# Latent products in another order, and finer waits in front of two output products, in a two-block transformer kernel

## What is computed

```python
proj = x @ w_in[l]        # na_q, na_k, na_v, df_q, df_k, df_v, m_cq (384), m_ckv (256), m_kr (32), gates
na_out  = neighbourhood_attention(...)              # 8 heads
df_out  = diff_attention(...)                       # 4 heads, two softmaxes each
q  = rms_norm(m_cq,  q_norm_g)  @ w_mla_qb          # latent attention, 8 heads
kv = rms_norm(m_ckv, kv_norm_g) @ w_mla_kvb         # gives k_nope and v
k  = concat(k_nope, rope(m_kr))
mla_out = softmax(rope(q) @ k.T * scale) @ v
merged = sum(sigmoid(gate_b) * (out_b @ w_branch[b]) for b in 0..2)
x = layer_norm(ALPHA * x + merged @ w_out)
hidden = silu(x @ w_gate) * (x @ w_up)              # 2816 wide
x = layer_norm(ALPHA * x + hidden @ w_ffn_out)
```

## Time and profile before

| | |
|---|---|
| median of 3 runs | 3397.44 us (3393.65 to 3398.08) |
| the profiled execution's own time | 3403.85 us |
| its span | 3402.0 us |
| mean granted TensorE clock | 0.966 of full |
| TensorE busy | 3179.8 us, 93% |
| VectorE, ScalarE, GpSimd busy | 41%, 31%, 10% |
| TensorE waiting for VectorE line 2703 / 2722 / 2579 (hidden) | 15.6 / 9.2 / 4.6 us, twice each |

### The profile page before, as it was taken

How to read it: one execution, slowest core, us unless ns; L and a number is a source line. 1 busy time by engine, 2 the same in 40 slices (tenths; PEclk the granted TensorE clock), 3 DMA queues, 4 the chain that set the end, 5 groups by cost and what they waited for, 6 DMA issues and landing times.

```text
span 3402.0 us, 38118 instructions
## 1 busy us (share of the span) xinstructions
PE 3179.8 (93%) x15140; PEld 2264.7 (67%) x15140; DVE 1388.2 (41%) x1857; ACT 1071.4 (31%) x1787; POOL 339.3 (10%) x269
## 2 busy tenths in 40 slices
PE   6989999979999979989999899998998999899996
PEld 3867777844444438765777688786775678678874
DVE  5676443341111054644334533334554433543334
ACT  3245332221001024445333322213444433232212
POOL 2455020000000011102100000000211110000000
PEclk9988999979999999999999999998999999999998
DMA  6012443459999942110212223233120122222221
GB/s 218 25 50 73 158 142 106 154 203 409 409 409 409 409 161 75 59 55 26 69 63 93 72 90 99 77 98 78 60 64 25 56 62 87 81 81 92 92 85 59
DMA packets 266257, 436.76 MB, mean 128 GB/s; under 512 B 9696, under 2 KB 180192, under 8 KB 265312
## 3 DMA queue, kind: packets, MB, share of 16 engines
q1 hardware_dynamic: 266080, 434.32, 36.2%
HBM read 432.19 MB, written 2.10 MB: 128 GB/s over the span
## 4 chain that ended last, share of the span: by engine, by line
PE 55%; DVE 5%; ACT 2%; DVEq 1%; issue 1%; ACTq 0%; POOLq 0%; DMA 0%; SPq 0%
PE bank L2247 46%; PE bank L2308 2%; PE bank L2325 2%; PE bank L2344 1%; PE bank L2284 1%; PE bank L1895 1%; DVE ring_r L2579 1%; PE bank L2339 1%; ACT ring_r L2448 1%; PE bank L2314 1%; DVE x L1926 1%; DVE layers_norm_rstd L1923 0%; DVE layers_work L2698 0%; DVE x_r L1937 0%; POOLq L2760 0%
## 5 line engine op out<-in xcount | busy, mean ns | idle before, releaser
L2247 PE MATMUL bank<-experts_x_hi_r,ring_r 128*128 128x512 f32 x1720 | 576.7, 400 | 7.0 <-DVE ring_r L2579 7.0
L2247 PE MATMUL bank<-x_r,ring_r 128*128 128x512 f32 x1376 | 546.2, 397 | 0.0
L2579 DVE TENSOR_TENSOR ring_r<-ring,ring_r 128x2048 fp32r<-128x2048 f32 (+2 forms) x162 | 324.9, 2006 | 421.0 <-ACT ring_r L2448 420.1
L2448 ACT ACTIVATE ring_r<-ring 128x2048 fp32r<-128x2048 f32 (+2 forms) x162 | 272.7, 1683 | 494.0 <-PE bank L2247 475.7
L2247 PE MATMUL bank<-layers_work_r,ring_r 128*128 128x512 f32 x1312 | 392.3, 401 | 9.2 <-DVE layers_work_r L2722 9.2
L2247 PEld LDWEIGHTS bank<-experts_x_hi_r,ring_r 128*128 128x128 f32 x1720 | 324.2, 188 | 109.5 <-issue 25.2
L2247 PE MATMUL bank<-ring_r 128*128 128x512 f32 (+1 forms) x1224 | 387.1, 377 | 0.0
L2247 PEld LDWEIGHTS bank<-layers_work_r,ring_r 128*128 128x128 f32 x1312 | 249.4, 190 | 78.6 <-DVE layers_work_r L2722 10.1
L2247 PEld LDWEIGHTS bank<-x_r,ring_r 128*128 128x128 f32 x1376 | 259.1, 188 | 62.9 <-issue 1.0
L2770 POOL TENSOR_TENSOR layers_p<-layers_p,layers_recip 128x512 f32<-128x512 f32 (+2 forms) x160 | 145.3, 925 | 1445.8 <-DVEq L2625 1445.8
L2247 PEld LDWEIGHTS bank<-ring_r 128*128 128x128 f32 x1224 | 223.5, 188 | 46.8
(11 more groups left out here) (399 smaller groups left out, 4827.1 us busy)
## 6 DMA issues: line engine op xcount, KB each, us to landing
ring<-in_w_in SPq DMA_DIRECT2D x74, 1024.0 KB, 5.3
ring<-in_w_ffn_in SPq DMA_DIRECT2D x44, 1024.0 KB, 5.1
mixer_kept<-in_w_up SPq DMA_DIRECT2D x33, 1024.0 KB, 18.3
mixer_kept<-in_w_down SPq DMA_DIRECT2D x28, 1024.0 KB, 18.5
mixer_kept<-in_w_gate SPq DMA_DIRECT2D x27, 1024.0 KB, 18.5
ring<-in_w_gate SPq DMA_DIRECT2D x24, 1024.0 KB, 18.4
ring<-in_w_down SPq DMA_DIRECT2D x23, 1024.0 KB, 18.4
ring<-in_w_ffn_out SPq DMA_DIRECT2D x32, 704.0 KB, 4.5
```

The lines of the kernel that those rows point to most:

```text
L2247: last = pe.matmul(out, lhs, rhs, start=start and k == 0, stop=stop and k == len(pairs) - 1)
L2448: act.activation(r32(whole(key, hi_at(i, key))), whole(key, raw_at(i, key)), ACT.Identity).then_inc(slab_round, 1)
L2579: dve.tensor_tensor(r32(tile), tile, r32(hi), ALU.subtract).then_inc(done, 1)
```

## The change

Three edits, in both layers.

1. The latent fills come in another order: features 4, 5, 3, 2, then msq kv, then features 0 and 1, the swap of the rotary key, msq q, then mv 0 and on as before. The slabs of these features are loaded in the order 2, 1, 0. msq kv waits for two squares instead of five, msq q for five. mv 0 waits for two of latent_done, and a new wait for all five stands before qn 0. The q root moves from tile 6 to tile 10 (mv 0 writes tile 6), and VectorE counts the roots in the new order. The events around a unit keep their places: a fill of the same number stands in the same slot. msq kv and feature 0 now follow the scores of unit (df, 2, 1), feature 1 and the swap those of (df, 2, 2), msq q and mv 0 those of (df, 2, 3).
2. wo 0 waits for six merged blocks, does their 18 passes, waits for all eight and does the last six passes.
3. fo 0 waits for 11 hidden blocks, and for all 22 in front of its second half.

```diff
--- before.py
+++ after.py
@@ -1970,7 +1970,8 @@
         v = toks("dfv", hh)
         return [a[0], a[1], q[0], b[0], q[1], b[1], k[0], v[0], k[1], v[1], v[2], v[3]]
 
-    latent = [("feat", "lat", m) for m in range(6)] + [("msq", "q"), ("msq", "kv"), ("swap", "kr", 0)]
+    lat = lambda *which: [("feat", "lat", m) for m in which]
+    latent = lat(4, 5, 3, 2) + [("msq", "kv")] + lat(0, 1) + [("swap", "kr", 0), ("msq", "q")]
     latent += [("mv", t) for t in range(TT)] + [("flip",), ("qn", 0), ("kn", 0), ("qr", 0), ("kn", 1), ("swap", "qr", 0)]
     queries = [("qn", 1), ("qr", 1), ("qn", 2), ("qn", 3), ("swap", "qr", 1), ("kn", 2), ("kn", 3)]
 
@@ -2019,7 +2020,7 @@
          "qn": (12, 14, 15, 18), "qr": (13, 10), "kn": (16, 17, 19, 21),
          "merged": (0, 1, 2, 3, 4, 20, 22, 23), "heads_hi": (24, 25, 26, 27), "merged_hi": (6, 7, 8, 9, 12, 13, 14, 15)}
 LAMBDA_AT = ("tok", "nav", 0, 0)
-LATENT_ROOT = {"q": 6, "kv": 9}
+LATENT_ROOT = {"q": 10, "kv": 9}
 WORK = 28
 
 
@@ -2103,7 +2104,7 @@
     source = {}
     for g, names in enumerate((("naq", "nak", "nav"), ("dfq", "dfk", "dfv"))):
         source |= {(n, hh): (W, 0, D, 512 * (3 * g + k) + 256 * hh, 256) for hh in (0, 1) for k, n in enumerate(names)}
-    source |= {("lat", c): (W, 0, D, L0 + 256 * c, 256) for c in range(3)}
+    source |= {("lat", c): (W, 0, D, L0 + 256 * c, 256) for c in (2, 1, 0)}
     source |= {("mla", 0): ("w_mla_2", 0, 3 * 768), ("mla", 1): ("w_mla_2", 3 * 768, 2 * D)}
     for b in range(3):
         for c in range(4):
@@ -2259,15 +2260,19 @@
                     return [(r32(a), r32(b)) for k in range(len(lhs))
                             for a, b in ((lhs[k], rhs[k]), (lhs[k], rhs_lo[k]), (lhs_lo[k], rhs[k]))]
 
-                def by_feature(key, c0, rhs, rhs_lo):
+                def by_feature(key, c0, rhs, rhs_lo, late=None):
 
                     slab = slabs_of(key)[0] if key[0] != "fu" else ("ffn", key[1])
                     need(slab)
                     hi, lo = parts(i, slab)
                     n = hi.shape[1]
                     banks.vacant(pe, key, i)
-                    chain(core.ps(key)[:, :], three([hi[:, k, c0:c0 + P] for k in range(n)], [lo[:, k, c0:c0 + P] for k in range(n)],
-                                                    rhs, rhs_lo)).then_inc(banks.put(key), 1)
+                    pairs, at = three([hi[:, k, c0:c0 + P] for k in range(n)], [lo[:, k, c0:c0 + P] for k in range(n)], rhs, rhs_lo), 0
+                    if late is not None:
+                        at = 3 * (n - 2)
+                        chain(core.ps(key)[:, :], pairs[:at], stop=False)
+                        pe.wait_ge(*late)
+                    chain(core.ps(key)[:, :], pairs[at:], start=at == 0).then_inc(banks.put(key), 1)
 
                 def couple(keys, fresh):
 
@@ -2387,11 +2392,13 @@
                         last.then_inc(banks.put(e), 1)
                     elif kind == "msq":
                         first, n, mat = (0, 3, "mean_q") if e[1] == "q" else (3, 2, "mean_kv")
-                        pe.wait_ge(latent_squared, i * LATENT + first + n)
+                        pe.wait_ge(latent_squared, i * LATENT + (2 if e[1] == "kv" else LATENT))
                         emit(e, [c2(mat)] * n, [tile("latent_sq", first + j) for j in range(n)])
                     elif kind in ("mv", "qn", "qr", "kn"):
                         need(("mla", 0), ("mla", 1))
                         if e == ("mv", 0):
+                            pe.wait_ge(latent_done, i * LATENT + 2)
+                        if e == ("qn", 0):
                             pe.wait_ge(latent_done, i * LATENT + LATENT)
                         wq, wkv = (flat[:, raw_at(i, ("mla", j)):raw_at(i, ("mla", j)) + n].rearrange("p (k n) -> p k n", k=k)
                                    for j, n, k in ((0, 3 * 768, 3), (1, 2 * D, 2)))
@@ -2410,9 +2417,9 @@
                                    [heads_out[:, e[1], k, :] for k in range(4)])
                     elif kind == "wo":
                         if e[1] == 0:
-                            pe.wait_ge(merged_split, i * KD + KD)
+                            pe.wait_ge(merged_split, i * KD + KD - 2)
                         by_feature(e, (e[1] % 2) * P, [tile("merged_hi", m) for m in range(KD)],
-                                   [tile("merged", m) for m in range(KD)])
+                                   [tile("merged", m) for m in range(KD)], (merged_split, i * KD + KD) if e[1] == 0 else None)
                     elif kind == "norm":
                         if e[1] == 1:
                             need()
@@ -2421,12 +2428,14 @@
                         by_feature(e, P * (kind == "fu"), x_hi, xs)
                     elif kind == "fo":
                         if e[1] == 0:
-                            pe.wait_ge(hidden_split, i * KF + KF)
+                            pe.wait_ge(hidden_split, i * KF + KF // 2)
                         banks.vacant(pe, e, i)
                         for hh in (0, 1):
                             need(("fo", e[1], hh))
                             hi, lo = parts(i, ("fo", e[1], hh))
                             n = KF // 2
+                            if e[1] == 0 and hh == 1:
+                                pe.wait_ge(hidden_split, i * KF + KF)
                             last = chain(core.ps(e)[:, :], three([hi[:, k, :] for k in range(n)], [lo[:, k, :] for k in range(n)],
                                                                  [hidden_hi(hh * n + k) for k in range(n)],
                                                                  [hidden(hh * n + k) for k in range(n)]),
@@ -2693,7 +2702,7 @@
                             dve.tensor_tensor(dst, dst, ssq[:, n, :].unsqueeze(2).broadcast_to([P, DF_HEADS, P]), ALU.mult)\
                                .then_inc(levelled, 1)
                     elif kind == "msq":
-                        dve.wait_ge(latent_root_done, i * 2 + (e[1] == "kv") + 1)
+                        dve.wait_ge(latent_root_done, i * 2 + (e[1] == "q") + 1)
                         root = work_tile(LATENT_ROOT[e[1]])
                         dve.reciprocal(root, root)
                         dve.drain()
```

## The result

The changed kernel takes 3368.62 us (median of four runs, 3366.52 to 3372.88) against 3397.4 for the one before (four runs): a ratio of 0.9919, 95% interval 0.9906 to 0.9931, or 27.5 us less with the interval 23 to 32; the two medians lie 28.8 us apart. The forecast was 3364.9, in a range of 3354 to 3381. The profiled execution of the changed kernel is the longest of its four, 3372.88 with a span of 3371.1 and a mean granted clock of 0.969 (before: 3403.85, span 3402.0, clock 0.966).

What follows compares the result with a forecast made beforehand. TensorE, busy 93% of the span, was taken as the bound, so only its gaps and half-clock stretches count. 18.7 + 8.9 + 4.9 = 32.5 us off the 3397.44 median gave 3364.9, range 3354 to 3381.

Steps and rivals of the forecast that it cites:

- The latent stage: Wait before the first latent product (mv) goes; 21.9 us available less two new waits of 1.6: gain 18.7, bounds 15.3 and 21.9.
- The combine at s + 11.9: VectorE ends unit (df, 2, 2)'s combine 11.9 us after s, the end of unit (df, 2, 3)'s scores on TensorE.
- I take nothing for the shorter gap: Latent stage: no clock loss counted behind the new 1.5 us gap at the transposes; 1.7 us each kept as other end.
- s + 5.30: Old trace's latent stage: VectorE's reciprocal starts 5.30 us after a unit's scores end, table load ahead of q root already counted.
- The first output product: Starts 2.81 us earlier, leaving a 1.8 us gap and a free second wait; 4.5 per layer, 8.9 us, bounds 5.6 and 10.6.
- I take half, 0.85: First output product: the remaining 1.8 us gap loses 1.7 us of clock or nothing, so 0.85 is counted per layer.
- The first down product: Its 2.28 us wait goes altogether, 2.4 with pipeline fill, with no clock lost: 4.9 us in both layers.
- A: Latent stage's q root binds harder and clocks drop, also at the output products: gain 24.6, 3372.8 us; chance 0.24.
- B: Latent wait only moved: transposes wait 5.5 us for the q part plus clock 2.7; gain 19.3, 3378 us; chance 0.08.
- C: Slower: granted clock falls because TensorE rests less; a fall of 0.03 gives 3421 us; chance 0.03.
- D: Edits don't act: another semaphore or bank releases TensorE at the same time; within 0.2%, 3397 us; chance 0.05.
- The bank wait: New TensorE waits for banks behind the latent stage would show the prediction wrong; banks hold narrowly, by half a microsecond.

Runs made afterwards that it cites:

- the down edit alone: Kernel before with only the first down product's wait changed (11 hidden blocks, 22 before its second half): 3393.05 us, ratio 0.9983.
- the latent edit alone: Kernel before with only the new order of latent fills and slabs and its waits: 3380.51 us against 3399.21, ratio 0.9947.
- the output edit alone: Kernel before with only the first output product's wait changed (six merged blocks, eight after 18 passes): 3390.91 us, ratio 0.9982.
- the finer wait without the distance: Kernel before with the two mean squares swapped, still side by side, mv 0 waiting for the key-value pair alone: 3397.84 us, ratio 0.9998.
- both together: Changed kernel, pending combine ahead of slab splits, rotary turns and latent roots, first output product waiting for five, six, eight merged blocks: 3353.00 us, ratio 0.9868.
- the combine was made earlier: Changed kernel with VectorE's pending combine done ahead of its wait for a latent root: 3367.38 us, ratio 0.9906, against 3368.62 for the changed kernel.

## Why the prediction was right

**The latent stage** was forecast at 18.7 us and gave 18.55 by the profiles and 18.0 by the edit alone. The steps hold one by one. "The wait is gone with 11 us to spare": 1503.8 against 1515.2, and with the kv root 3.35 us longer still nothing waits. "The combine at s + 11.9", TensorE there at "s + 10.4": s is 1512.55, the combine ends at 1524.48, s + 11.93, and TensorE's gap starts at 1523.13, s + 10.6, since the last product's way through the pipeline wasn't in my count. Hence 1.40 where the prediction had "a new wait of 1.5 to 1.6 us". "I take nothing for the shorter gap" of the clock: right in all gaps of 1.40 that the runs show. The last was a choice, and the earlier trace rows would have allowed 1.7 each. There is some luck in the agreement: the forecast of 21.9 us for the whole stage rests on the half clock of one execution, and against the profile of the down edit alone the stage gained 16.1 us, not 18.55.

**The table loads.** The root's load and the root itself in after (ScalarE's timeline):

```profile
1516.25 1.28 ACT L2537 ACT_TABLE_LOAD   x1
1517.55 0.69 ACT L2537 ACTIVATE layers_work<-bank,con 128x512 f32<-128x512 f32 x1
```

There are four more loads, as said: by groups, lines 2508 and 2537 have 6 and 4 of them where 2499 and 2528 had 4 and 2 in before. A load is 1.28 us and the root starts 0.02 us behind it; the combine ends where the count without a drain had it. The Trainium skill (ScalarE: Activation LUTs, What ACT_TABLE_LOAD costs) gives the load right, and its drain of about 1380 ns, which would have made the wait 3.0 us, isn't in this row. The prediction's "3.0 us" was not a fair use of it in any case: s + 5.30 was read from a row that already had a load ahead of the q root, and whatever came with it. The advice of the Trainium skill (ScalarE: Activation LUTs, Table sets: the hidden batching unit) to batch calls by set would have spoken against an edit that brings 18 us. The two extra loads per layer cost nothing here: that of the kv root lies where its pair is ready 11 us early, and each load back to the exponential ends before the maximum is there.

**The first output product** was forecast at 8.9 and gave 5.6 + 1.8 = 7.4 by the profiles, 6.1 (3 to 9) by the edit alone. The start (2.81 earlier), the remaining gap (1.8, here 1.79) and the free second wait hold. The mis-sized term is the clock: "I take half, 0.85". In after the clock fell behind both gaps and cost 1.55 each. By the half-and-half term the loss in two layers would be 1.7, it is 3.1. That is nearly the whole miss of this part. The loss behind the old gap, 2.5 a layer, was one execution's too: behind the same 4.6 us the output products take 49.92 and 49.98 us in before, 50.17 and 50.12 with the down edit alone, but 49.06 and 49.05 with the latent edit alone, as long as behind the gap of 1.79 in after. Over the seven kernels that have this gap of 1.79 it was lost 10 times in 14. The two products of one kernel can differ, as the output edit alone shows, and with one term of 1.55 for each a chance of 0.7 would have been the better value. The end of 5.6 that the prediction named still holds.

**The first down product**: forecast 4.9, 4.86 by the profiles, 5.8 (3 to 9) by the edit alone. Nothing was late next.

**The sum** was 32.5, and the touched stages gave 30.8. From its own time the prediction was 3371.3, and the profiled execution took 3372.88. Forecast and median are 3364.9 and 3368.6, 3.7 apart: 1.7 of that is the sum, the rest is where the profiled executions stood among their runs. The forecast took the half clock of an execution 6.4 us above its median off the median itself, where less of it may stand.

**The rivals.** A (q root binds harder, clocks drop, 3372.8) is partly true: the drop of the clock at both output products happened, the longer wait and the drop in the latent stage didn't. It would have cost 4.57 us of wait and 2.0 to 2.6 of clock had the q root been 3.35 longer. B (wait only moved, 3378) is false for the change and true for its half, the finer wait without the distance. C (granted clock falls because TensorE rests less) is false: it rose from 0.966 to 0.969 (0.964 to 0.972 over the runs of before, 0.969 to 0.973 over those of after), and in the fastest version (both together), with the waits gone, 143 us through the latent stage ran at 1.00:

```profile
1398.00:1541.00 143.00, 142.05 (x733) 100.24 (x731) 79.42 (x146) 78.57 (x181) 21.20 (x23) 1.00 0.17 53
```

D (the edits don't act) is false by each one of the three alone. The bank wait named as the sign of an error didn't come in after; it came, 0.63 us long, as soon as the combine was made earlier.

## What to carry to other kernels

A wait for several results of an in-order queue is shortened by making the wanted one early, with other work between it and its reader; asking for fewer of them moved the wait to the next reader and gained nothing measurable. Look at what stands behind a long step in the queue: a 0.75 us operation put ahead of roots, splits and swaps was worth 11 to 12 us here. When a gap is only shortened, ask whether the clock comes back: going from 4.6 to 1.79 us paid for the gap and at most part of the clock, going on to 0.40 paid for both. A clock loss read from one execution is a draw, not a constant: look at the same gap in several profiles before it goes into a sum.

## What the runs showed of the hardware

**Gaps and the clock.** Over all thirteen profiles the same gaps recur, and each was or wasn't followed by half clock, seen as a granted clock below 0.8 over the 5 us from the gap's end:

```
TensorE gap                                    followed by half clock
0.40 us, inside the first output product         0 of  4
1.40 us, transposes, latent stage                0 of 10
1.75 us, gate products, not all three edits      7 of 20
1.75 us, gate products, with all three edits     0 of 32
1.79 us, first output product                   10 of 14
2.28 us, first down product                      0 of  8
2.75 us, transposes ahead of the latent stage   22 of 22
```

At the first output product the loss is 1.55 us or nothing, so such a gap costs itself or nearly twice itself; behind 4.57 us at the transposes it was 2.0 and 2.6. The length of the gap alone doesn't decide: 2.28 us never cost the clock, though 1.79 mostly did. What TensorE did before differs: the down product's gap comes behind a stretch of 235 us without any gap, at 1.00. What decides is not shown. Nor is it shown why the gate products' gap lost the clock only in kernels that don't carry all three edits; 7 of 20 against 0 of 32 is hardly chance, and at 1.6 us each it may be a small gain that the stages above leave out. Half clock behind these gaps makes up part of the differences between executions of one kernel; that it makes up all of them is only argued.

**A fallen clock can be hidden by the next gap.** With the two mean squares side by side, 'mv' 0 took 1.96 us behind its gap of 2.40 in the first layer and 3.15 in the second (TensorE's timeline, second layer):

```profile
2578.07 3.15 PE L2247 MATMUL bank<-ring,layers_work 128*128 128x512 f32 x4 [2.40 <-DVE layers_work L2705]
2583.95 1.11 PE L2325 MATMUL bank<-con,layers_p 128*128 128x128 f32 x4 [2.73 <-DVE layers_p L2636]
```

Half clock ate 1.19 us, and the wait behind it is 2.73 instead of 3.92, 1.19 less. From 'mv' 0 to the transposes it is 5.88 us in the second layer, 5.87 in the first. VectorE sets the end, so the lost clock costs nothing there.
